# Two attention loops of a four-layer kernel re-ordered: grouped attention's query strips moved one place ahead, the older head's sums moved inside the key strip

## What is computed

```
s = einsum("bhcqd,bhckd->bhcqk", q, k)
p = softmax(s)
attn = p[:, :, 0] - lam * p[:, :, 1]
o = einsum("bhqk,bhkv->bhqv", attn, v)
o = rms_norm(o, subln_g) * (1.0 - lam_init)
y = (o * silu(g)) @ w_out
```

```
q = rope(rms_norm(q, q_norm_w))
k = rope(rms_norm(k, k_norm_w))
attn = softmax(q k^T * d**-0.5) v
y = concat([sgu * silu(za), attn * silu(zb)]) @ w_out
```

## Time and profile before

| what | value |
|---|---|
| median of 3 runs | 2805.18 us (2803.17 to 2805.68) |
| the profiled execution's own time | 2805.79 us |
| its span, first to last instruction | 2804.1 us |
| mean granted TensorE clock in it | 0.977 |
| PE matmul busy | 2639.0 us, 94% of the span |
| DVE busy | 2045.8 us, 73% |
| ACT busy | 1224.6 us, 44% |
| POOL busy | 211.6 us, 8% |
| HBM traffic | 177 GB/s over the span |

### The profile page before, as it was taken

One profiled execution on the slowest core, in us unless ns is written; L12 is line 12 of the kernel. 1 busy time (PEld: TensorE's weight loads), 2 busy tenths in 40 slices (PEclk: granted clock), 3 DMA queues, 4 the chain that ended last, 5 costly groups with the idle time before them and its releaser, 6 DMA issues.

```text
span 2804.1 us, 39539 instructions
## 1 busy us (share of the span) xinstructions
PE 2639.0 (94%) x13490; PEld 2133.3 (76%) x13490; DVE 2045.8 (73%) x3196; ACT 1224.6 (44%) x1875; POOL 211.6 (8%) x402
## 2 busy tenths in 40 slices
PE   5799999999899999999989899999998997999989
PEld 1477777788677777777768788888886887998978
DVE  4399999999778788687877777764454666775655
ACT  3266556622443444444345433323444324544642
POOL 1110011011000000000000011100000100110000
PEclk8799999999999999999999899999999998999999
DMA  9765455476455565565655355532221643873325
GB/s 370 287 196 164 166 181 177 145 262 225 180 180 204 178 199 181 183 209 195 217 187 193 131 188 182 187 123 99 68 74 49 223 148 124 282 239 120 122 101 167
DMA packets 126557, 498.35 MB, mean 178 GB/s; under 512 B 14464, under 2 KB 16512, under 8 KB 116608
## 3 DMA queue, kind: packets, MB, share of 16 engines
q1 hardware_dynamic: 74176, 267.49, 27.7%
q0 software_dynamic: 52288, 229.66, 23.8%
HBM read 492.90 MB, written 4.19 MB: 177 GB/s over the span
## 4 chain that ended last, share of the span: by engine, by line
PE 75%; DVE 12%; issue 5%; DMA 4%; ACT 3%; DVEq 1%; POOL 0%; ACTq 0%; POOLq 0%; SPq 0%
PE psum L249 18%; PE psum L251 18%; PE psum L250 18%; PE psum L262 4%; DMA y<-in_mod_weights 2%; DVE w_lo L231 2%; PE psum L263 2%; DVE psum L409 2%; PE psum L299 2%; ACT w_hi L223 1%; PE psum L1631 1%; PE psum L1099 1%; PE psum L836 1%; DVE work L411 1%; PE psum L1645 1%
## 5 line engine op out<-in xcount | busy, mean ns | idle before, releaser
L249 PE MATMUL psum<-h_both,w_hi 128*128 128x512 f32 (+1 forms) x3264 | 1184.3, 363 | 5.6 <-DVE w_lo L231 5.6
L251 PE MATMUL psum<-h_both,w_lo 128*128 128x512 f32 (+1 forms) x3264 | 1156.1, 354 | 0.0
L250 PE MATMUL psum<-h_both,w_hi 128*128 128x512 f32 (+1 forms) x3264 | 1155.4, 354 | 0.0
L231 DVE TENSOR_TENSOR w_lo<-raw,w_hi 128x1024 fp32r<-128x1024 f32 x496 | 584.9, 1220 | 305.3 <-ACT w_hi L223 302.4
L249 PEld LDWEIGHTS psum<-h_both,w_hi 128*128 128x128 f32 x3264 | 619.6, 190 | 100.0 <-issue 13.2
L250 PEld LDWEIGHTS psum<-h_both,w_hi 128*128 128x128 f32 x3264 | 619.8, 190 | 92.4 <-issue 9.8
L251 PEld LDWEIGHTS psum<-h_both,w_lo 128*128 128x128 f32 x3264 | 619.1, 190 | 85.8
L223 ACT ACTIVATE w_hi<-raw 128x1024 fp32r<-128x1024 f32 x496 | 496.7, 1052 | 388.3 <-PE psum L251 301.4
L262 PE MATMUL psum<-h_both,w_hi 128*128 128x512 f32 x480 | 177.0, 409 | 10.0 <-DVE h_both L609 9.6
L263 PE MATMUL psum<-h_both,w_lo 128*128 128x256 f32 x480 | 137.0, 286 | 0.0
L409 DVE SCALAR_TENSOR_TENSOR psum<-y,modraw 128x1024 f32<-128x1024 f32 x98 | 120.3, 1228 | 21.1 <-DMA y<-in_mod_units 18.5
(11 more groups left out here) (289 smaller groups left out, 3127.3 us busy)
## 6 DMA issues: line engine op xcount, KB each, us to landing
raw<-in_weights SPq DMA_DIRECT2D x496, 512.0 KB, 4.4
y<-in_mod_units POOLq DMA_DIRECT2D x130, 512.0 KB, 4.2
modraw<-in_mod_weights POOLq DMA_DIRECT2D x48, 1024.0 KB, 5.5
work<-in_mod_units POOLq DMA_DIRECT2D x62, 512.0 KB, 4.6
y<-in_mod_weights POOLq DMA_DIRECT2D x16, 1024.0 KB, 9.1
xl<-in_mod_units POOLq DMA_DIRECT2D x32, 512.0 KB, 4.8
modraw<-in_mod_units POOLq DMA_DIRECT2D x32, 512.0 KB, 4.7
modraw<-in_cond_rows POOLq DMA_DIRECT2D x6, 1024.0 KB, 8.0
```

Source lines behind the costliest of these rows:

```text
L231: dve.tensor_tensor(w_lo[:, par, half, :], raw[:, 2 * par + half, :], w_hi[:, par, half, :].bitcast(F32), ALU.subtract).then_inc(S["split_ ...
L249: pe.matmul(dst, hi, h_hi[:, k, 0:n], start=(k == 0), stop=False)
L250: pe.matmul(dst, hi, h_lo[:, k, 0:n], start=False, stop=False)
L251: mm = pe.matmul(dst, lo, h_hi[:, k, 0:n], start=False, stop=(k == KT - 1))
```

## The change

It has five parts. (a) In the norms of layers 1 to 3, DVE reads the reciprocal root from PSUM, and ACT's copy is made for layer 0 only. (b) In layer 1's attention, head i-2's sum of squares runs between the two halves of head i's key strip. Its square root then stands first in ACT's round, followed by a one-column exponential. (c) Grouped attention is rewritten: the stream's order becomes q0, q1, z0, q2, z1, ... q7, z6, z7 (z is a gate strip), each round has head i's query strip and head i-1's gate strip, one drain round is left instead of two, and a head's transposes and weighted values come one round sooner. The queries' eviction stands ahead of the split. (d) At the end of both grouped attentions, the first out tiles are split between the last head's parts, and PE runs tiles 0 and 1 strip by strip. (e) SP waits for 28 used modulation loads instead of 24. The helpers `q_strip`, `z_strip`, `turned` (rotation), `scores`, `sums`, `turned_weights` (transposes), `weighted`, `exps`, `weights` (ACT's eviction of the transposed weights), `gate`, `softmax`, `normed`, `rotated` and `gated` hold the same instructions as before, under new names.

```diff
@@ norm_sqrt, norm_dve
             if l > 0:
                 split_hi(act, layer_strip[l] // 2, 1, halves=(0,))
-            act.wait_ge(S["rstd_ps"], l + 1)
-            act.activation(nb["rstd"], psum[:, SS_BANK, :], ACT.Copy).then_inc(S["rstd_done"], 1)
+            else:
+                act.wait_ge(S["rstd_ps"], 1)
+                act.activation(nb["rstd"], psum[:, SS_BANK, :], ACT.Copy).then_inc(S["rstd_done"], 1)
...
-            dve.wait_ge(S["rstd_done"], l + 1)
+            dve.wait_ge(S["rstd_ps"], l + 1)
...
-                                         in1=nb["rstd"][:, 0:T], op0=ALU.mult, op1=ALU.mult)
+                                         in1=psum[:, SS_BANK, 0:T], op0=ALU.mult, op1=ALU.mult)
@@ out_first
-                    pe.wait_ge(S["split_lo"], 2 * (out_strip[l] + 1) + half + 1)
+                    pe.wait_ge(S["split_lo"], 2 * (out_strip[l] + strips[-1]) + half + 1)
@@ att_pe
+                def sums():
+                    pe.wait_ge(A["o_evac"], i - 1)
+                    pe.wait_ge(A["sdq"], min(i, HEADS1) if isinstance(i, int) else i)
+                    pe.matmul(psum[:, M_BANK, 0:T], ones, osq, start=True, stop=True).then_inc(A["sso"], 1)
+
+                def key_strip(half):
+                    if half:
+                        mod_chunk(pe, M_ATT + j, 2 * par)
+                    elif older:
+                        sums()
...
-                    strip(pe, att_strip(j, par, 0), psum[:, K_BANK, :], NT, chunk(0))
+                    strip(pe, att_strip(j, par, 0), psum[:, K_BANK, :], NT, key_strip)
...
-                if older:
-                    pe.wait_ge(A["o_evac"], i - 1)
-                    pe.matmul(psum[:, M_BANK, 0:T], ones, osq, start=True, stop=True).then_inc(A["sso"], 1)
+                if older and not here:
+                    sums()
@@ att_act
+                def root():
+                    act.wait_ge(A["sso"], i - 1)
+                    act.activation(osq, psum[:, M_BANK, 0:T], ACT.Sqrt, scale=1.0 / P, bias=eps_col).then_inc(A["sdo"], 1)
+                if older and here:
+                    root()
+                    act.activation(warm, eps_col, ACT.Exp)
...
-                if older:
-                    act.wait_ge(A["sso"], i - 1)
-                    act.activation(osq, psum[:, M_BANK, 0:T], ACT.Sqrt, scale=1.0 / P, bias=eps_col).then_inc(A["sdo"], 1)
+                if older and not here:
+                    root()
@@ gqa_pe: the new round
             def body(j, par):
                 i = 2 * j + par
+                here, before = live(i, HEADS2), live(i - 1, HEADS2)
+                first, second, end = (isinstance(i, int) and i == m for m in (0, 1, HEADS2))
+                if here:
+                    ge(pe, B["q_evac"], base + i)
+                    strip(pe, q_strip(lay, j, par), psum[:, 0, 0:n], n, (lambda half: None if half else turned(0)) if second else None)
+                if second:
+                    scores(0, 0)
+                if before and not second and not end:
+                    turned_weights(i - 1)
+                if here:
+                    sums(i)
+                if before:
+                    ge(pe, B["sz"], base + i - 1)
+                    strip(pe, z_strip(lay, j, par), psum[:, 1, 0:n], n)
+                if second or end:
+                    turned_weights(i - 1)
+                if end:
                     pe.wait_ge(B["q_evac"], base + HEADS2)
                     pe.wait_ge(B["sz"], base + HEADS2)
-                    out_first(pe, 2 + lay, 0, 4)
+                    out_first(pe, 2 + lay, 0, 2, strips=(0,))
+                    out_first(pe, 2 + lay, 0, 2, strips=(1,))
+                    out_first(pe, 2 + lay, 2, 5)
+                if here and not first:
+                    turned(i)
+                if before:
+                    weighted(i - 1, 1 - par)
+                if here and not first:
+                    scores(i, par)
                 if end:
...
+                    out_first(pe, 2 + lay, 5, OUT_REST)
+            rounds(pe, body, HEADS2, 1, 4)
@@ gqa_act: the new round
+                if before and not second:
+                    exps(i - 1)
+                if here:
+                    st = q_strip(lay, j, par)
+                    act.wait_ge(S["strip_done"], st.s + 1)
+                    ge(act, B["qr"], base + i)
+                    if first:
+                        act.wait_ge(B["v_t"], 2 * (lay + 1))
+                    act.activation(q2s[:, 0:n], psum[:, 0, 0:n], ACT.Square)
+                    act.activation(q2[:, 0:n], psum[:, 0, 0:n], ACT.Copy).then_inc(B["q_evac"], 1)
+                    next_strip(split_hi, act, st)
+                if second:
+                    exps(0)
+                if before and not second and not end:
+                    weights(i - 1)
+                if here:
+                    act.wait_ge(B["ssq"], base + i + 1)
+                    act.activation(q2s[:, 0:n], psum[:, 6, 0:n], ACT.Sqrt, scale=1.0 / P, bias=eps_col).then_inc(B["sdq"], 1)
                 if before:
...
+                    st = z_strip(lay, j, par)
                     act.wait_ge(S["strip_done"], st.s + 1)
+                    if end:
+                        to_high(act, 2 + lay, 0, 2)
+                        split_hi(act, st.pair + 1, st.par, halves=(0,))
+                        weights(i - 1)
+                        to_high(act, 2 + lay, 2, 4)
+                        split_hi(act, st.pair + 1, st.par, halves=(1,))
+                        gate(i - 1, 1 - par)
+                        to_high(act, 2 + lay, 4, OUT_REST)
+                    else:
+                        if second:
+                            weights(0)
+                        next_strip(split_hi, act, st)
+                        gate(i - 1, 1 - par)
@@ gqa_dve: the new round
+                if second:
+                    rotated(0)
+                if before and not second:
+                    softmax(i - 1)
+                if here:
+                    next_strip(split_lo, dve, q_strip(lay, j, par))
+                if second:
+                    softmax(0)
+                if here:
+                    normed(i)
+                if here and not first:
+                    rotated(i)
                 if end:
+                    st = z_strip(lay, j, par)
+                    to_low(dve, 2 + lay, 0, 2)
+                    split_lo(dve, st.pair + 1, st.par, halves=(0,))
+                    to_low(dve, 2 + lay, 2, 4)
+                    split_lo(dve, st.pair + 1, st.par, halves=(1,))
+                    gate(i - 1, 1 - par)
+                    to_low(dve, 2 + lay, 4, 6)
+                    gated(i - 1, 1 - par)
+                    to_low(dve, 2 + lay, 6, OUT_REST)
+                elif before:
+                    next_strip(split_lo, dve, z_strip(lay, j, par))
+                    gate(i - 1, 1 - par)
+                    gated(i - 1, 1 - par)
@@ sync
-            sp.wait_ge(S["mod_used"], 4 * (MOD_FIRST - 2))
+            sp.wait_ge(S["mod_used"], 4 * (MOD_FIRST - 1))
@@ _stream
-             + [c for h in heads for c in (q + h, zb + h)])
+             + [q + heads[0]] + [c for n in range(1, HEADS2) for c in (q + heads[n], zb + heads[n - 1])] + [zb + heads[-1]])
```

More of the change, by code:

```diff
@@ new lines, in sums, with turned_weights @@
+            def sums(h):
+                pe.wait_ge(B["q_evac"], base + h + 1)
+                ge(pe, B["sdq"], base + h)
+                pe.matmul(psum[:, 6, 0:n], ones, q2s[:, 0:n], start=True, stop=True).then_inc(B["ssq"], 1)
+            def turned_weights(h):
+                pe.wait_ge(B["attn"], base + h + 1)
+                for qt in range(2):
+                    for kt in range(4):
+                        mm = pe.transpose(psum[:, 2 + qt, kt * P:(kt + 1) * P], p2[qt][:, kt * P:(kt + 1) * P], ident)
+                if wide_:
+                    for qt in range(2):
+                        for kt in range(2):
+                            mm = pe.transpose(psum[:, 4, kt * T + qt * P:kt * T + (qt + 1) * P],
+                                              p2[2][:, qt * T + kt * P:qt * T + (kt + 1) * P], ident)
+                mm.then_inc(B["attn_t"], 1)
@@ L1587, in body @@
             def body(j, par):
                 i = 2 * j + par
-                here, before, older = live(i, HEADS2), live(i - 1, HEADS2), live(i - 2, HEADS2)
-                last, end = (isinstance(i, int) and i == HEADS2 + n for n in range(2))
-                if last:
+                here, before = live(i, HEADS2), live(i - 1, HEADS2)
[3 more added lines that the diff above has]
+                    strip(pe, q_strip(lay, j, par), psum[:, 0, 0:n], n, (lambda half: None if half else turned(0)) if second else None)
@@ L1617, in body @@
-                if here:
-                    ge(pe, B["sz"], base + i)
-                    strip(pe, gqa_strip(lay, j, par, 1), psum[:, 1, 0:n], n)
-                    pe.wait_ge(B["q_evac"], base + i + 1)
```

(23 more changed lines are left out.)

258 lines of the change are left out of this document (105 added, 153 removed).

## The result

The changed kernel takes **2776.28 us** (median of 4 runs, 2774.55 to 2780.49) against 2805.36 for the kernel before in the same session: ratio 0.990, 95% interval 0.9883 to 0.9917, or 29.1 us less (23 to 33). Timed again beside the last experiments it gave 2777.69, ratio 0.9902 (0.9885 to 0.9919). Forecast were 2788.0, 17.2 less, in a range of 2774 to 2799: sign and range held, but the gain is 1.7 times what my sum gave, and the sum is what has to be explained. The profiled execution took 2780.49 (span 2778.8), 4.2 above the median, so the two profiled executions differ by 25.3 only.

The account below looks back on a forecast made before the run. PE's work plus PE's pauses bound the kernel (PE busy 94%), and no PE work is removed. Terms -17.9 (b), -1.1 (a), +1.0 (e), +0.8 (c, d) sum to -17.2 from 2805.18: 2788.0 us, range 2774 to 2799.

Parts of the forecast that it names:

- rival 1: Ends of grouped attention: the last gate does not hold PE, 8.4 less and 4.5 of clock; 2775 us, 14%.
- minus 18.6: Layer 1's attention: the 14 pauses at L1114, 18.6 us together, vanish with early sums and the root first on ACT.
- The insertion: Layer 1's attention: the sums' small matmul inside the key strip costs 0.05 us extra a round, plus 0.7.
- Rival 2: Layer 1's attention: the inserted sums cost their own switch, 0.48 x 14 = 6.7 us more; 2795, 11%.
- rival 3: Layer 1's attention: the L1114 pause stays, because `k_evac` or `sdq` ends just behind `sdo`; 2806, 5%.
- The cover: Layer 1's attention: two more ACT table loads a round, 1.28 us each, fall where ACT waits; otherwise up to 1.28 a round.
- The gains put down: Norms of layers 1, 2 and 3: DVE's first scaling gains 0.26, 0.9 and 0 us; sum given as minus 1.1.
- +1.0: The start: SP's four later loads go out next to the last modulation load and start later; plus 1.0 us.
- +0.8: Grouped attention, both layers: new pauses 31.0 us against old 30.2, clock loss unchanged; plus 0.8, bounds minus 13 and plus 10.
- the old loss of 8.1: Grouped attention: the clock below full speed took 8.1 us in the old kernel, assumed to stay.
- Rival 5: Out tiles behind grouped attention: the long end pause lowers the clock for all of them, +33 less 4.5; 2816, 4%.
- Rival 4: ACT in grouped attention: each table change costs twice its row, about 11 us more; 2799, 4%.

Follow-up runs that it names:

- b_rootlate: The kernel before with part b alone, but ACT's root left at its old place and no one-column exponential; loop of 14 rounds 656.87 us against 648.71 before.
- experiment 2: Part b alone (loop 627.27 us) run without the one-column exponential (627.25), and also with the root at its old place (656.87); kernel before 648.71.
- part a alone: The kernel before with only the norm hunks of the diff; 2802.68 us against 2804.96, ratio 0.9995 (0.9981 to 1.0008).
- tiles_together: The changed kernel, but PE takes the first five out tiles with both strips at once; end pauses 6.3 and 5.1 us, as in the changed kernel.
- end_gate_early: The changed kernel with the last head's gate before the splits, the weights' eviction earlier, PE's gate wait after the first strip's two tiles; 2769.38 us in one execution.

## Why the prediction was right, and where it was not

**Sign, place and order were right.** Part b carries the change, L1114's pause is gone, and the pauses that parts c and d leave stand where the prediction had put them. That the time fell into the range is partly luck: 2776.3 lies near its lower end, which stands on rival 1, and rival 1 is false. What moved the time there is part b, larger than its term, and parts c and d, which gained where a loss stood.

**Part b was mis-sized: -21.4, not -17.9.** The step that failed is "minus 18.6". I took the gap as drawn. In the earlier trace rows the last matmul before it begins at 1055.52, and the strip as a whole took 7.43 us; the same strip without the pause takes 5.84. The pause was worth 1.59 and 0.08 at the switch behind it, not 1.33. In parts c and d I had added 0.16 for each pause; here, where there were 14, I had not. The insertion, put at 0.05, was 0.47 - 0.34 = 0.13: the bound of 0.5 from the earlier trace rows was close to the price of the matmul in the strip, and the argument that the old place cost much the same held. Rival 2 (0.48 more a round, nothing given back) is refuted by the 0.34; rival 3, the pause stays, happened only in b_rootlate, and by a cause that the rival doesn't name: neither `k_evac` nor `sdq` but the root's place.

**The cover held.** I had said that the two table loads would fall into ACT's idle time. They do (experiment 2), and the one-column exponential that was to move one of them is worth 0.0 (627.25 against 627.27).

**Part a: the size held, its split over the layers did not.** The gains put down, 0.26, 0.9 and 0, sum to 1.2, not 1.1. From L493 to PE's next L288 it took 5.21, 5.88 and 5.01 us in layers 1, 2 and 3 before, and 5.24, 5.24 and 4.76 in the changed kernel: gains of 0, 0.64 and 0.25. But the same stretch of layer 1 is 4.96 to 5.88 in the six profiled kernels that have the copy, and 4.71 to 5.24 in the eight executions without it. The means differ by 0.20, 0.77 and 0.18, together 1.15. So the 0.41 and the 0.15 of the earlier trace rows were one draw each, and 0.15 was no floor: layer 3 gained too, and the wait for PE's own matmul, 0.45 in layer 2, lies above it. The median of part a alone, -2.3, has no change inside its interval and so decides nothing.

**Part e: nothing in the medians**, where +1.0 stood. The profiled executions show what the prediction named as the loss, the last modulation load longer by 2.6, where it had allowed 2.4 at most. Of its rows one was read wrong: the four loads took 8.1 to 14.3 us to land, and the 4.6 is of a load that was issued at 142.2 us. Why the medians show nothing stays open.

**Parts c and d: -5.3 in the profiled executions and -3.2 in their median, not +0.8.** Idle time fell by 3.7 us and PE's busy time by 1.6. The old idle time, 26.6, was read right; the sum then has a slip (26.6 and 20 times 0.16 is 29.8, not 30.2), and the wide end and the narrow layer have 15 such pauses, not 20. The new ones came to 22.9 us idle and not 31.0, and this is the larger error. Term by term, forecast then drawn: first rounds wide 4.7 and 3.4, narrow 6.3 and 4.7; rounds wide 0.6 and none, narrow 5.5 and 3.1; ends wide 7.6 and 6.3, narrow 6.3 and 5.2. The step that failed most is the table load that I counted before head 0's root and before head 7's gate. Neither exists: the keys' root leaves the root's table loaded, and head 7's gate follows head 7's exponentials with no root between them. At the wide end that is 1.28 of the 1.3 that are missing, at the narrow one 1.28 where 1.1 are missing; at head 0's rotations DVE's split of the next strip, which ends at 1892.3 and 2540.2, held the reciprocal instead, so there part of the 1.28 only was gained. The Trainium skill ("ScalarE: Activation LUTs", section "Table sets: the hidden batching unit") lists tanh beside exp in one set, and square root in another; the trace agrees, and I had not looked there. In the narrow rounds I had 0.8 and the rotation's wait is drawn as 0.51, worth 0.78.

**The clock.** I kept the old loss of 8.1. PE's busy time in the two layers fell by 0.9 and 0.7. Rival 5, the low clock for all the out tiles, is refuted: 4.83 us at 1.2 GHz behind the pause of 6.27, 3.4 behind the pause of 5.1 in the narrow layer, and full clock from there on. The warning in the Trainium skill ("TensorE: Matmul & The Clock Gate", section "HAM oscillation — how this bites in real kernels"), that the piece behind a pause starts slow, shows at this place, and end_gate_early bounds its price: 1.9 us of the 7.1 are left when the shorter pauses are taken off, and half of 4.83 is 2.4.

**Rival 1** gave nearly the measured time, 2775, and is false: tiles_together and end_gate_early show that the gate did hold PE. That its number fits is chance. **Rival 4**, each table change costs twice, is refuted: in each of the 14 traces 62 to 84 activations start 1.29 us behind the start of their load, as in b_rootlate's rows (1054.49 and 1055.78), and all that start later waited for PE, DVE or a transfer.

## What to carry to other kernels

Price a recurring pause by the same piece of work with and without it, not by the gap as drawn: the gap left out 0.25 us each time, 3.5 us over 14 rounds. When PE waits for another engine's queue, ask which item in the queue it needs first: here a gate of 0.6 us behind 5 us of splits and evictions held PE, and only reordering gave 7 and 4 us. Before a table load is put into a chain, go back to the last root, exponential or tanh that ran on ACT. Before a difference between two profiles is put down to an edit, look at the same place in a second profile of the same kernel: here 1.6 us at one norm and 1.1 in layer 3 were gone in it.

## What was unexpected of the hardware

An inserted matmul of another weight costs 0.47 us inside a strip of 512 columns, of which 0.34 comes back at the place it left. A short pause before a matmul costs 0.25 to 0.27 us more than it is drawn (1.59 for 1.34, 0.78 for 0.51). The clock's low stretches at one place differ between two executions of one kernel (10.2 and 17.1 us at layer 2's norm), and this alone moves a stage by 1.6 us; what decides it stays open. With SP's four loads beside it the last modulation load takes 14.4 to 14.8 us instead of 11.2 to 12.5, and the medians still don't show it.
